# Two pooling gate tiles moved into the paged stage of a hybrid decoder step

## The reference, cut to what matters

```python
h = rms_norm(x, norm_mix)
q, k, v, u, ga, gp = jnp.split(h @ w_in, SPLITS, axis=-1)      # each 1024 columns wide
o = attention_fn(q, k, v, lam)            # prompt: causal; samples: cached pages + 8 new keys
pool_o, pool_state = pool_mixer(u, ...)   # windows 2, 4, 8, 16: d = window mean - u; d @ w_pool[g]
merged = sigmoid(ga) * (o @ w_attn_branch) + sigmoid(gp) * (pool_o @ w_pool_branch)
x1 = x + merged @ w_out                   # then the channel mixer
```

## Time and profile before

| | |
|---|---|
| median of 3 runs | 2094.36 us (2093.21 to 2094.56) |
| the profiled execution's own time | 2096.5 us |
| its span, first to last instruction | 2094.7 us |
| PE busy | 2041.9 us, 97% of the span |
| DVE, ACT, POOL busy | 1125.2, 615.3, 487.0 us |
| mean granted TensorE clock | 0.985 of full speed |
| DMA | 187.74 MB, mean 90 GB/s |

### The profile page before, as it was taken

How to read it: one execution, slowest core, us unless ns; L and a number is a source line. 1 busy time by engine, 2 the same in 40 slices (tenths; PEclk the granted TensorE clock), 3 DMA queues, 4 the chain that set the end, 5 groups by cost and what they waited for, 6 DMA issues and landing times.

```text
span 2094.7 us, 33677 instructions
## 1 busy us (share of the span) xinstructions
PE 2041.9 (97%) x13113; PEld 1858.2 (89%) x13113; DVE 1125.2 (54%) x1499; ACT 615.3 (29%) x1216; POOL 487.0 (23%) x339
## 2 busy tenths in 40 slices
PE   9999999999988878999999999999999999999999
PEld 8888888888867766999999988999999999999997
DVE  6766666665632433366553434555555455555556
ACT  5444544445411111224112322221221122122120
POOL 4333333332100000342332111211221122022110
PEclk9999999999988989999999999999999999999999
DMA  4222212124499996312224410110121111112112
GB/s 151 57 62 57 62 41 57 33 62 132 121 271 281 273 285 211 92 41 61 87 80 135 150 37 25 57 42 31 51 62 31 41 51 41 31 51 62 31 41 97
DMA packets 189120, 187.74 MB, mean 90 GB/s; under 512 B 11680, under 2 KB 154540, under 8 KB 188852
## 3 DMA queue, kind: packets, MB, share of 16 engines
q1 hardware_dynamic: 155068, 142.42, 23.1%
q10 hardware_dynamic: 33920, 43.43, 7.0%
HBM read 161.68 MB, written 24.35 MB: 89 GB/s over the span
## 4 chain that ended last, share of the span: by engine, by line
PE 93%; DMA 4%; DVE 1%; SPq 1%; ACT 0%; ACTq 0%; issue 0%; POOL 0%; POOLq 0%; DVEq 0%
PE PS L1498 39%; PE PS L2265 13%; PE PS L1032 6%; PE PS L2020 5%; PE PS L288 4%; PE PS L290 4%; PE PS L289 4%; PE PS L344 3%; DMA v_pg<-in_cache_v_dram 3%; PE PS L368 3%; PE PS L357 2%; PE PS L1102 1%; PE PS L1136 1%; PE PS L1519 1%; PE PS L1531 1%; PE PS L323 1%
## 5 line engine op out<-in xcount | busy, mean ns | idle before, releaser
L1485 POOL TENSOR_TENSOR fw_lo<-fw_raw,fw_hi 128x1024 fp32r<-128x1024 f32 x86 | 216.1, 2512 | 941.4 <-ACT fw_hi L1481 941.4
L1498 PE MATMUL PS<-m_hi,fw_hi 128*128 128x384 f32 (+1 forms) x1032 | 228.1, 329 | 0.0
L1498 PE MATMUL PS<-m_lo,fw_hi 128*128 128x384 f32 (+1 forms) x1032 | 227.4, 328 | 0.0
L1498 PE MATMUL PS<-m_hi,fw_lo 128*128 128x384 f32 (+1 forms) x1032 | 227.4, 328 | 0.0
L2393 DVE TENSOR_TENSOR x<-x,PS 128x512 f32<-128x512 f32 x198 | 136.2, 688 | 142.8 <-PE PS L2265 142.5
L1498 PEld LDWEIGHTS PS<-m_hi,fw_lo 128*128 128x128 f32 x1032 | 176.3, 188 | 0.0
L1498 PEld LDWEIGHTS PS<-m_lo,fw_hi 128*128 128x128 f32 x1032 | 176.2, 188 | 0.0
L1498 PEld LDWEIGHTS PS<-m_hi,fw_hi 128*128 128x128 f32 x1032 | 175.9, 188 | 0.2
L288 PE MATMUL PS<-w_hi,act_hi 128*128 128x384 f32 (+1 forms) x456 | 164.7, 361 | 0.0
L290 PE MATMUL PS<-w_hi,act_lo 128*128 128x384 f32 (+1 forms) x456 | 153.6, 337 | 0.0
L289 PE MATMUL PS<-w_lo,act_hi 128*128 128x384 f32 (+1 forms) x456 | 153.1, 336 | 0.0
(11 more groups left out here) (318 smaller groups left out, 4220.5 us busy)
## 6 DMA issues: line engine op xcount, KB each, us to landing
k_ring<-in_cache_k_dram SPq DMA_DIRECT2D x256, 128.0 KB, 4.4
v_pg<-in_cache_v_dram ACTq DMA_DIRECT2D x51, 512.0 KB, 11.2
fw_raw<-in_w_up_dram SPq DMA_DIRECT2D x44, 512.0 KB, 4.1
wd_raw<-in_w_down_dram SPq DMA_DIRECT2D x22, 512.0 KB, 4.2
w_raw<-in_w_in_dram SPq DMA_DIRECT2D x21, 512.0 KB, 5.2
out_dram<-raw SPq DMA_DIRECT2D x16, 512.0 KB, 3.7
fw_raw<-in_w_in_dram SPq DMA_DIRECT2D x12, 512.0 KB, 4.0
fw_raw<-in_w_in_dram ACTq DMA_DIRECT2D x12, 512.0 KB, 8.0
```

Of the source, the lines that this page charges most:

```text
L1485: e.tensor_tensor(fw_lo[slot][:, 0:kts, :], fw_raw[:, 0:kts, :], fw_hi[slot][:, 0:kts, :].bitcast(F32), ALU.subtract).then_inc(fw_tail, 1)
L1498: ins = e.matmul(PS[:, 3 * slot + c, 0:cw], w[slot][:, kt, :], x[:, kt, c0:c0 + cw], start=first and kt == 0, stop=last and kt == KT - 1)
```

## The change

`N_FP` becomes 8: all gp tiles are fill of the paged stage, which then has 48 chunks instead of 42, and 38 instead of 32 behind `P_FIRST`. The samples get 7, 5, 5, 5, 5, 4, 4, 3. A sample's chunks are split anew: two beside the softmax as before; one (`P_PROBS`) between the turned probabilities and the value pages; of the rest, half (rounded down) between pages 3 and 4; the others at the end. For 7, 5, 4 and 3 chunks that is 2+1+2+2, 2+1+1+1, 2+1+0+1 and 2+1+0+0 (before: 2+0+1+3 for six, 2+0+1+2, 2+0+1+1, 2+0+1+0 for five, four, three, and 2 for two). ACT and PE change alike.

In stage 3 the two gate tiles, their weight loads, splits and sigmoids out of PSUM go; ACT takes the sigmoid of `sig_p` for all 8 tiles. Four spilled gp tiles instead of two come back with L1931. The first load of `w_pool` is issued right behind the last `u` weights, ahead of the stores of `u_rows`; its split follows in the `u` loop (the tile numbers 24 and on have stayed). The DVE wait for the stores of `u_rows` moves to the tile of `po_lo` that lies over `u_rows`.

```diff
-        N_FP = 6
+        N_FP = KT
         N_FILL = N_FP + KT
-        N_U, N_GP, N_PL, N_PB, N_AB, N_UP = N_FILL, N_FILL + KT, 3 * KT, 4 * KT, 5 * KT, 6 * KT
+        N_U, N_PL, N_PB, N_AB, N_UP = N_FILL, N_FILL + KT, 4 * KT, 5 * KT, 6 * KT
-        P_EACH = (6, 5, 4, 4, 4, 4, 3, 2)
+        P_EACH = (7, 5, 5, 5, 5, 4, 4, 3)
+        P_PROBS = 1
+        def split_chunks(fill):
+            mid = 2 + P_PROBS + (len(fill) - 2 - P_PROBS) // 2
+            return fill[0:2], fill[2:2 + P_PROBS], fill[2 + P_PROBS:mid], fill[mid:]
...
         def pe_phase2(e):
...
                 pe_probs(e, b)
+                for f in after_probs:
+                    f()
                 for j in range(KEY_GROUP):
                     pe_value_page(e, b, j)
-                for f in fill[2:3]:
+                for f in between:
                     f()
                 for j in range(KEY_GROUP, NPG + 1):
                     pe_value_page(e, b, j)
-                for f in fill[3:]:
+                for f in rest:
                     f()
...
         def act_phase2(e):
...
-                act_chunk(e, fill[1])
+                act_chunk(e, first[1])
+                for p in after_probs:
+                    act_chunk(e, p)
                 act_load_values(e, b, 0, KEY_GROUP)
...
         def pe_phase3(e):
...
-            pe_fm_tile(e, N_GP, 0, act_hi, act_lo)
             u_rows_transpose(KT - 1)
-            pe_fm_tile(e, N_GP + 1, 1, act_hi, act_lo)
             e.wait_ge(ur_copied, KT)
             pe_o_transposes(e, 0, NSAMP)
...
-                if m < N_FP:
-                    e.activation(sig_p[:, m, :], sig_p[:, m, :], ACT.Sigmoid)
-            fm_head(e, N_GP + 1, 1)
-            gate(N_GP, KT - 2, 0)
+                e.activation(sig_p[:, m, :], sig_p[:, m, :], ACT.Sigmoid)
             act_u_rows(e, KT - 1)
...
-            fm_head(e, N_PL, 0)
-            gate(N_GP + 1, KT - 1, 1)
...
-            e.wait_ge(ur_st, UR_STORES * 16)
             for m in range(KT):
+                if m == PO_OVER_U_ROWS:
+                    e.wait_ge(ur_st, UR_STORES * 16)
...
-            fm_tail(e, N_GP + 1, 1)
             pool_rstd_o(e, step, 0)
-            for k in range(POOL_LOADS):
-                fm_tail(e, N_PL + k, k)
+            fm_tail(e, N_PL + 1, 1)
...
-            for i in range(2):
-                fm_load(e, N_GP + i, w_in_cols(COL_GP + (N_FP + i) * P))
+            for k in range(POOL_LOADS):
+                (wait fw_tail, load w_pool: moved here from below the stores of u_rows)
             e.wait_ge(ur_copied, KT)
             e.dma_start(pool_prompt[0, 0], u_rows[NSAMP:NSAMP + BUF, :]).then_inc(ur_st, 16)
```

More of the change, by code:

```diff
@@ L1149, in pe_phase2 @@
             for b in range(NB):
-                fill = [lambda p=p: pe_chunk(e, p, {}) for p in chunks_of(b)]
+                first, after_probs, between, rest = split_chunks([lambda p=p: pe_chunk(e, p, {}) for p in chunks_of(b)])
                 pe_new_scores(e, b)
@@ L1153, in pe_phase2 @@
                 if b == 0:
-                    fill[0]()
+                    first[0]()
                 pe_page_scores(e, b, 1)
                 if b:
-                    fill[0]()
-                fill[1]()
+                    first[0]()
+                first[1]()
                 pe_probs(e, b)
+                for f in after_probs:
+                    f()
                 for j in range(KEY_GROUP):
                     pe_value_page(e, b, j)
-                for f in fill[2:3]:
+                for f in between:
                     f()
@@ L1194, in act_phase2 @@
             for b in range(NB):
-                fill = chunks_of(b)
+                first, after_probs, between, rest = split_chunks(chunks_of(b))
                 if b == 0:
-                    act_chunk(e, fill[0])
+                    act_chunk(e, first[0])
                 act_sample_exp(e, b)
                 if b:
-                    act_chunk(e, fill[0])
-                act_chunk(e, fill[1])
+                    act_chunk(e, first[0])
+                act_chunk(e, first[1])
+                for p in after_probs:
+                    act_chunk(e, p)
                 act_load_values(e, b, 0, KEY_GROUP)
-                for p in fill[2:3]:
+                for p in between:
                     act_chunk(e, p)
@@ L1206, in act_phase2 @@
                 act_take_values(e, b)
-                for p in fill[3:]:
+                for p in rest:
                     act_chunk(e, p)
@@ L1383, in build_step @@
         sp_rows = r("sp_rows", [NB * BUF, D])
+        PO_OVER_U_ROWS = (r.at - R2U) // fit(TOK)
         u_rows = r("u_rows", [NSAMP + BUF, D])
@@ L1935, in sp_phase3 @@
                 fm_load(e, N_U + m, w_in_cols(COL_U + m * P))
-            for i in range(2):
-                fm_load(e, N_GP + i, w_in_cols(COL_GP + (N_FP + i) * P))
+            for k in range(POOL_LOADS):
+                e.wait_ge(fw_tail, N_PL + k)
+                e.dma_start(fw_raw[:, :, :].rearrange("p (k a) b -> p k (a b)", a=2),
+                            w_pool[0, 2 * k:2 * k + 2].rearrange("g (kt p) n -> p (g kt) n", p=P)).then_inc(fw_ld, 16)
             e.wait_ge(ur_copied, KT)
@@ L1941, in sp_phase3 @@
                 e.dma_start(pool_sample[0, b, BUF - NS:BUF, :], u_rows[b * NS:(b + 1) * NS, :]).then_inc(ur_st, 16)
[L1942 to L1945, removed]
             for m in range(2):
```

## The result

The changed kernel takes 2116.66 us, median of 4 runs (2108.5 to 2118.41), against 2093.78 (2090.0 to 2094.56) for the kernel before in the same comparison: ratio 1.0105, 95% interval 1.0076 to 1.0135. It is slower by about 23 us. The forecast was 2090.0 with a range of 2081 to 2100, so time and sign were both wrong.

The account below looks back on a forecast made before the run. The prediction took the paged stage as bound by transfers and the rest by PE. Paged stage +5.7, start of stage 3 -3.5 and +0.5, behind the last `u` tile -7.1 gave -4.4 us: 2090.0, range 2081 to 2100.

Parts of the forecast that it names:

- Sample 7: Paged stage, no wait for a page: grows by a whole chunk less the hidden probability copy, +3.2 us (+2.8 to +3.9).
- sample 6: Paged stage: a slow chunk at the end and later pages, less faster scores and less page competition, +3.5 us (+2 to +6).
- -3.5 and +0.5: Stage 3: the `sp_rows` wait and its slow stretch go, -3.5 us; later weights of the third `u` tile cost +0.5.
- the sums: DVE's three window sums behind the last `u` tile: 2.1 us shorter without POOL's split of tile 23 beside them.
- the clock: Pooling maps behind the last `u` tile: PE, having stood still some 15 us, starts at the lower clock, +1.6 us.
- samples 0 to 5: Paged stage: samples 1 to 4 -3.6, sample 5 +1.5, sample 0 -1, volume +2.5; about -1 us (-8 to +19).
- The landing need not slip by 3.2: Samples 1 to 5: page 7 lands 25.0 to 25.5 us after the scores' end (S), despite issue 3.2 us later.
- what is queued: Allowance of 1.5 to 2 us in page 7's landing time for transfers already queued.
- Later issue, later landing: Third rival: samples 0 to 6 each grow 3.2 us, +22.4, total 2110; half gives 2098.7; chance 0.13, whole or half.
- Pages 4 to 6 are then mostly there: Samples 1 to 4: shorter stall and half the clock loss gone, periods of 35.0 us, a gain of 0.9 each.
- none between pages 3 and 4, so PE waits there: Sample 5: four chunks kept, PE waits between the pages and stays slow, 36.0 us against 34.5, +1.5.
- The first sentence: Claim that the paged stage is bound by transfers with PE partly idle; DMA share about 1 in samples 0 to 5.

Follow-up runs that it names:

- e3: Kernel before, 42 chunks and its stage 3 kept; one chunk placed behind the turned probabilities, the rest split as in the change: 2110.75 us, ratio 1.0091.
- e1: Changed kernel, 48 chunks, at the old places: two beside the softmax, none behind the probabilities, one between value pages 3 and 4, rest at the end: 2108.08 us.
- e14: Changed kernel with one chunk moved from behind page 7 to between pages 3 and 4 in samples 1 to 6, early chunk kept: 2084.76 us, ratio 0.9934.
- e4: Kernel before, 42 chunks, split two beside the softmax, none behind the probabilities, two between pages 3 and 4, rest at the end: 2082.82 us, ratio 0.9946.
- e6: Kernel before, 42 chunks, split one beside the softmax, none behind the probabilities, three between pages 3 and 4, rest at the end: 2083.85 us, ratio 0.9957.
- e7: Changed kernel, 48 chunks, split two beside the softmax, none behind the probabilities, three between pages 3 and 4, rest at the end: 2091.6 us, ratio 0.9986.
- e8: Changed kernel, 48 chunks, split one beside the softmax, none behind the probabilities, three between pages 3 and 4, rest at the end: 2092.9 us, ratio 0.9991.

## Why the prediction was wrong

**Right.** The issue of pages 5 to 7 was to slip by 3.2 us; it went from S + 14.3 to S + 17.7 on average over samples 1 to 5, +3.3. Sample 7 was to grow by 3.2, it grew by 3.6; sample 6 by 3.5, it was 2.2. Up to the last `u` tile stage 3 was to gain 3.0 (-3.5 and +0.5) and gained 3.8. Behind it the sums were to fall by 2.1, and fell from 6.48 to 4.38; the first map was to come 8.7 earlier, it was 8.6; the clock was to cost 1.6 on the maps, it was 1.3, with a granted clock of 0.74 behind the gap. Together these terms were forecast at +3.5 + 3.2 - 3.0 - 7.1 = -3.4 and measured at +2.2 + 3.6 - 3.8 - 8.6 + 1.3 = -5.3.

**Wrong: one term, samples 0 to 5, -1 forecast and +18.9 measured.** The step that failed is "The landing need not slip by 3.2", an overlap that did not take place. The text reasoned that the keys would be issued by S + 20.7, that the pages would then have the engines to themselves, and put page 7 at S + 25.0 to 25.5. Measured: S + 26.3, 28.8, 27.8, 29.4, 28.4 for samples 1 to 5, average 28.1, against 23.5 before. Of these 4.6 us, 3.3 are the issue and 1.3 a longer flight: 10.5 us against 9.2, and 10.2 in e3 over the same five samples. Samples 1 to 4 were forecast at 35.0 and average 38.9. Of these 3.9 us, 2.8 are the landing (28.1 against the middle of the forecast, 25.25); the other 1.1 is the work between landing and the end of the values, 1.9 us in each sample of the chain and not the 0.85 that was left for it. The starting point was off as well: S + 24.3 for page 7 before supposes one chunk behind it in every sample, but sample 1 has two, and the traces give 23.5.

Sample 5 shows what the working left out. The last key was issued at S + 20.6, as forecast. From then to the landing of page 7, 7.8 us later, the two queues moved (packets, MB, share):
```profile
q10 hardware_dynamic: 402, 1.49, 68.7%
q1 hardware_dynamic: 437, 0.72, 35.5%
```
q10 carries what ACT issues and q1 what SP issues. So keys that were issued were not yet out of the way: 0.72 MB passed on their queue after the last issue. From the issue of page 5 at S + 15.4 to the landing of page 7 it was 3.6 MB in 13.0 us, 2.5 MB on ACT's queue, where the three pages are 1.57; ACT had issued the weights of a tile, 0.52 MB, 1.2 us ahead of them. The forecast counted 1.57 MB, half as much again for keys, and 1.5 to 2 us for "what is queued". That is the term that was too small.

**The rival that happened** is the third, "Later issue, later landing", which was to decide from S + 27 and gave each period of samples 0 to 6 +3.2, +22.4 together. Measured +21.0. It was given 0.13 with its half. The argument against it, that the keys are out of the way by S + 20.7, did not hold, as sample 5 shows.

That the two sums agree so well is partly luck. The rival has page 7 slip by 3.2 in each sample and each period grow with it. In samples 2 to 4, where one chunk stands behind page 7 as before, that is about what came (periods +3.0, +3.2, +4.1). In sample 1 the landing slipped by 4.2 and the period grew by 0.2, with one chunk less behind the page. In sample 0 the landing slipped by 2.8, there is one chunk less too, and the 3.2 us that PE stood still at the end of its scores make up most of the +2.7; their cause is open. In sample 6 page 7 did not slip at all (S + 24.0 against 24.3), and the +2.2 goes with the chunk added behind it.

**What the forecast overlooked** is that the split decides, not the number. "Pages 4 to 6 are then mostly there" counted the chunk ahead of page 0 as cover. It isn't: pages 0 to 3 have landed by then (the chain has no wait at them), so the chunk only delays the uses that free the ring. e3 shows that cost alone (+15), e1 the cost of chunks behind page 7 (+13 with the 11 won in stage 3 already in it), and e14 that the loss vanishes (-34) once the chunk behind moves between the pages, with the early one still in its place. Sample 5 is the purest case: the same four chunks, none left between the pages, a landing 5.5 us later and a period 5.8 us longer. The forecast saw that ("none between pages 3 and 4, so PE waits there") and priced it at +1.5.

**The first sentence too was only half right.** The forecast took the stage to be bound by transfers because its shares were near 1, and concluded that delay at the issue would be absorbed. e4 carries the same bytes in 242.5 us at 283 GB/s where before took 255.4 at 268: there was 5% of slack, which a better order could take and a worse one widen. A share near 1 was true of the flights, and not of the stretch ahead of them.

By the Trainium skill, DMA: Bandwidth & Descriptors, section "Issuing engines are not separate DMA queues", all issuing engines feed the same 16 DMA engines. The trace agrees: in the two queue rows of sample 5 above ACT's and SP's queues have 68.7% and 35.5% of the engines, together 104%, which is full by this measure. e4, e6, e7 and e14, at shares of 0.97 to 1.02, all move 280 to 283 GB/s. The rule tells nothing of the changed kernel's 255 GB/s, which is a matter of issue.

**Where the gain of the move went.** With the stage at 280 GB/s, 48 chunks take 251.3 us (e14) and 42 take 242.5 (e4) over samples 0 to 6, +8.8, of which the 2 MB more are about 7 at that rate; sample 7 adds 3.6. The move wins 11.1 in stage 3 (3.8 + 8.6 - 1.3). So on these figures it is worth nothing on this kernel, and e14 and e4, at 2084.8 and 2082.8 with intervals that overlap, are not told apart.

## What to carry to other kernels

When a ring of buffers is refilled as it is used, place filler work behind the uses that release the refills and ahead of the first use of what was refilled. Here a filler ahead of the releases delayed the whole chain, and one behind the last arrival was paid in full. Before you price a delayed issue at less than its length, look at the DMA share in two windows, the flight itself and the stretch ahead of the issue: where the engines are full in the flight and have gaps ahead of it, the delay passes through. Count all bytes in the queues, too, also those issued before. And compare bytes over time for the stage with the best rate any window shows: a mean share of 0.95 still hid 13 us.

## What the runs showed of the hardware

**Flight time of a queued page.** A value page of 512 KB took about 10 us from its issue to its landing (averages over samples 0 to 6 of the last page that PE waited for, nearly always page 7: 9.8 before, 9.9 after, 9.8 in e3). Against the mean share of its sample's period it shows no trend (10.84 us at 0.82 in sample 5 after the change, 8.17 at 0.97 before). The mean hides where the gaps are. Within the flights of samples 0 to 5 the share is 1.02 to 1.06 in all three kernels, so the flight is work of full engines: 10.84 us at 280 GB/s are 3.0 MB. Only sample 6 differs: 6.38 us at 0.83 after the change, 6.46 at 0.98 in e3, but 9.94 at 0.86 before. Where the engines are full all along, as in e6 to e8, the flights in the chain are 10.5 to 19.0 us. I had expected the flight to end soon after the keys were issued; it lasted some 8 us longer, with the engines full. Which bytes passed ahead of the page is not shown.

**DVE beside POOL.** The three window sums took 6.48 us beside POOL's 3.59 us split and 4.38 without it, the same instructions. The split took longer too, 3.59 us where it took 2.40 beside the third `u` tile. The Trainium skill, SBUF — State Buffer, section "SBUF: two separate sides", says that VectorE and GpSimd take their shared port pair in turn, for a whole instruction. The trace agrees in that both were slowed and the sums lost 2.10 us, less than the length of one split; it does not show the turns themselves. Here the 2.10 us shortened the path by themselves.
